# Layer norms of two hybrid layers: GpSimd applies the learned scale and offset for all tiles but the last two of each layer

## The chip, the cores and the metric

One core of a Trainium2 chip. The metric is the device time of one execution in microseconds (us), lower is better. The kernel before takes 3786.14 us, the median of 3 runs.

## The reference, cut to what matters

Four layers run one after the other on 1024 tokens of width 1024: an attention layer, a state-space layer, and two hybrid layers. The change is at the end of each hybrid layer, where the mixed branches `y` are projected and the result is normalised:

```python
def layer_norm(x, g, b):
    xf = x.astype(F32)
    mu = jnp.mean(xf, axis=-1, keepdims=True)
    var = jnp.mean(jnp.square(xf - mu), axis=-1, keepdims=True)
    return ((xf - mu) * lax.rsqrt(var + LN_EPS) * g + b).astype(x.dtype)

def hybrid_layer(...):
    ...
    y = jnp.concatenate([y_conv, y_ret, y_na], axis=-1) @ w_out
    x_new = layer_norm(DEEPNORM_ALPHA * x + gate[:, None] * y, ln_g, ln_b)
    if not need_ctx:
        return x_new, None
    ...
    yc = jnp.concatenate([yc_conv, yc_ret, yc_na], axis=-1) @ w_out
    xc_new = layer_norm(DEEPNORM_ALPHA * xc + mod_c[2] * yc, ln_g, ln_b)
    return x_new, xc_new
```

`ln_g` and `ln_b` have 1024 values each, one per column, the same for every token. Layer 0 normalises 1024 tokens and 256 context tokens, layer 1 the 1024 tokens alone. All data is fp32.

## The kernel before

Rows of tokens lie on the 128 partitions, so a tile is 128 tokens by 1024 columns. Layer 0 (`l == 0`) has 10 tiles (8 of tokens, 2 of context), layer 1 has 8. A projection in fp32 is three matmul passes, over high and low parts of both operands; GpSimd makes the two parts of each slab of weights (`split`, lines 2312 and 2315; `keep`, lines 2425 and 2427, for the six slabs that stay resident), each a 128x1024 instruction.

Each engine runs a program of its own, in the order in which it is written, and waits for semaphores. For the end of a hybrid layer these are `ln_pe`, `ln_act` and `ln_dve`; GpSimd has no part in it. It has finished the slabs of `w_out` by then, and its next work is `split` for the first two slabs of the layer that follows, which waits until the last tile's matmuls have freed their buffers.

**TensorE** (`ln_pe`). `res_first` multiplies tiles 0 to 3 together. Then, in layer 0: tile(4), turn(0), turn(1), tile(5), turn(2), turn(3), tile(6), turn(4), tile(7), turn(5), tile(8), turn(6), tile(9), turn(7), turn(8), turn(9). `tile(t)` is one tile's projection (line 416, 48 matmuls) and from tile 6 on waits for the gating product of tile t-2 (`f_scaled`), which frees its PSUM banks. `turn(t)` is eight transposes of the normalised tile (line 446); it waits for the tile's sum (`f_sum`) and, from tile 2 on, for both takes of tile t-2. In layer 1 there is no turn: tile(4) to tile(7) follow at once.

**VectorE** (`ln_dve`). `gated(t)` is L2083, product of the projection in PSUM and the gate; L2087, plus ALPHA times x with the row sums; L2090, minus the mean. L2087 waits for the rows of x (`f_loaded`). From tile 4 on L2083 waits until the store of tile t-2 has landed. `normed(t)` is L2095, reciprocal of the root; L2097, add and multiply by the two row statistics; L2099, times the learned scale; L2101, plus the learned offset. `take(t)` (L471) and `rest(t)` (L478) write the transposed tile for the next layer.

**ScalarE** (`ln_act`). `square(t)` is L2001, the sum of squares, and L2004, the root. `store(t)` waits for `f_sum`, issues the tile's store (L2009) and, behind it in the same queue, the load of x for tile t+2 (L1996):

```python
def store(t):
    act.wait_ge(f_sum, base + t + 1)
    act.dma_start(orows(t), L_T[:, t % 4]).then_inc(f_stored[t % 2], 16)
    if t + 2 < tiles:
        load_x(t + 2)
```

Its order in both layers starts square(0), square(1), store(0), square(2), store(1), square(3), store(2), store(3). Layer 0 goes on with take(0), take(1), then square(4), take(2), store(4), square(5), take(3), store(5) and so on; a take on ScalarE is L456 and the cast L461. Layer 1 goes on with square(4), store(4), square(5), store(5) and so on.

VectorE's order in both layers starts gated(0), gated(1), normed(0), gated(2), normed(1), gated(3), normed(2), normed(3). Layer 0 goes on with take(0), rest(0), take(1), rest(1), then gated(4), take(2), normed(4), rest(2) and so on. Layer 1 goes on with gated(4), normed(4), gated(5), normed(5) and so on.

Of the kernel before, what the change touches and what calls it, by code (L numbers as in the profile page):

```python
# [16 lines left out]
ALU = mybir.AluOpType  # L17
# [8 lines left out]
NT = S // P  # L26
# [102 lines left out]
T_DONE, F_DONE, Y_DONE = 2 * NT, 2 * NT, KT  # L129
CONST_DONE, FC_DONE = 5, 2  # L130
# [3 lines left out]
def build(nc, io, out):  # L134
    x_in = io["x"].rearrange("b s d -> (b s) d")
    ctx = ExitStack()
    with ctx:
# [3 lines left out]
        def sem(name):  # L141
            return ctx.enter_context(nc.semaphore(name))
# [22 lines left out]
        def region(at, *shape):  # L165
            n = int(np.prod(shape))
            assert at + n <= ARENA, (at, shape)
            v = arena[:, at:at + n]
            if len(shape) == 2:
                v = v.rearrange("p (a b) -> p a b", a=shape[0])  # L170
            if len(shape) == 3:
                v = v.rearrange("p (a b c) -> p a b c", a=shape[0], b=shape[1])
            return v
# [186 lines left out]
        def y_dve(dve, base, src, order8, cols=S):  # L360
# [9 lines left out]
        f_const = sem("f_const")  # L370
        r_mul, f_square, f_root, f_rstd, f_scaled, f_sum = [
            sem(n) for n in ("r_mul", "f_square", "f_root", "f_rstd", "f_scaled", "f_sum")]
# [12 lines left out]
        def ps_tile(j):  # L385
            return psum[:, 2 * j:2 * j + 2, :].rearrange("p a c -> p (a c)")
# [52 lines left out]
        def pair_of(t):  # L439

            return ps_tile(t if t < 4 else t % 2)
# [21 lines left out]
        def take_dve(dve, n, first, gain, full=N_FULL):  # L463

            b = n % 2
            dve.wait_ge(t_turned, n + 1)
            if n >= first + 2:
                dve.wait_ge(t_hi, n - 1)
                dve.wait_ge(t_lo, n - 1)
            for k in range(4, 8):  # L470
                ins = nc.vector.tensor_scalar(full[:, b, k * P:(k + 1) * P], ps_tile(2 + b)[:, k * P:(k + 1) * P],  # L471
                                              gain[:, 0, k:k + 1], gain[:, 1, k:k + 1], ALU.mult, ALU.add)
            ins.then_inc(t_full_dve, 1)

        def rest_dve(dve, n, c0, full=N_FULL):

            dve.wait_ge(t_hi, n + 1)
            nc.vector.tensor_tensor(act_lo[:, :, c0:c0 + P], full[:, n % 2].rearrange("p (k c) -> p k c", k=KT),  # L478
                                    act_hi[:, :, c0:c0 + P].bitcast(F32), ALU.subtract).then_inc(t_lo, 1)
# [1453 lines left out]
        L_T = region(2048, 4, 1024)  # L1933
        RES_L = resident("res_l", *(10240 + 2048 * i for i in range(6)))
        F_GATE = region(22528, 2, 1024)
        F_LN = region(24576, 2, 1024)
# [1 line left out]
        F_SQ = region(28672, 1024)  # L1938
        F_ST2 = region(29696, 4, 8)
        ALPHA = 4.0 ** 0.25  # L1940
        f_chain, f_norm = sem("f_chain"), sem("f_norm")
        def ln_rows(tok, con):
            return lambda t: tok[t * P:(t + 1) * P, :] if t < NT else con[(t - NT) * P:(t - NT + 1) * P, :]

# [46 lines left out]
        def ln_act(act, l, xrows, orows):  # L1991
# [72 lines left out]
            for b in range(2):  # L2064
                act.wait_ge(f_stored[b], 16 * ((base + tiles) // 2))

        def ln_dve(dve, l):

            V = nc.vector
            base, n0 = F_DONE + 10 * l, T_DONE + 10  # L2070
            r0 = 3 * NT + 10 * l

            def half_of(t):
                return pair_of(t) if l == 0 else ps_tile(t % 4)

            def gated(t):
                m, st = base + t, F_ST2[:, t % 4]
                dve.wait_ge(r_mul, r0 + t + 1)
                if t >= 4:
                    dve.wait_ge(f_stored[t % 2], 16 * (m // 2))  # L2080
                    if l == 0:
                        dve.wait_ge(t_turned, n0 + t - 3)
                V.tensor_tensor(L_T[:, t % 4], half_of(t), F_GATE[:, 0 if t < NT else 1], ALU.mult).then_inc(f_scaled, 1)  # L2083
                dve.wait_ge(f_scaled, m + 1)
                dve.wait_ge(f_loaded[t % 2], 16 * (m // 2 + 1))
                k = 2 * (m - F_DONE)
                V.scalar_tensor_tensor(L_T[:, t % 4], L_X[:, t % 2], ALPHA, L_T[:, t % 4], ALU.mult, ALU.add,  # L2087
                                       accum_out=st[:, 0:1]).then_inc(f_chain, 1)
                dve.wait_ge(f_chain, k + 1)
                V.tensor_scalar(st[:, 1:2], st[:, 0:1], -1.0 / D, None, ALU.mult).then_inc(f_chain, 1)  # L2090

            def normed(t):
                m, st = base + t, F_ST2[:, t % 4]
                dve.wait_ge(f_root, m + 1)
                V.reciprocal(st[:, 5:6], st[:, 4:5]).then_inc(f_rstd, 1)  # L2095
                dve.wait_ge(f_rstd, m + 1)
                V.tensor_scalar(L_T[:, t % 4], L_T[:, t % 4], st[:, 1:2], st[:, 5:6], ALU.add, ALU.mult).then_inc(f_norm, 1)  # L2097
                dve.wait_ge(f_norm, 2 * (m - F_DONE) + 1)
                V.tensor_tensor(L_T[:, t % 4], L_T[:, t % 4], F_LN[:, 0], ALU.mult).then_inc(f_norm, 1)  # L2099
                dve.wait_ge(f_norm, 2 * (m - F_DONE) + 2)  # L2100
                V.tensor_tensor(L_T[:, t % 4], L_T[:, t % 4], F_LN[:, 1], ALU.add).then_inc(f_sum, 1)  # L2101

            def take(t):
                take_dve(dve, n0 + t, n0, G_X if t < NT else G_C, L_FULL)

            def rest(t):
                rest_dve(dve, n0 + t, t * P, L_FULL)

            dve.wait_ge(f_const, 16 * (FC_DONE + 4 * (l + 1)))
            gated(0)  # L2110
            gated(1)
            normed(0)
            gated(2)
            normed(1)
            gated(3)
            normed(2)
            normed(3)
            if l == 0:
                take(0)
                rest(0)  # L2120
                take(1)
                rest(1)
                gated(4)
                take(2)
                normed(4)
                rest(2)
                gated(5)
                take(3)
                normed(5)
                rest(3)  # L2130
                gated(6)
                take(4)
                normed(6)
                rest(4)
                gated(7)
                take(5)
                normed(7)
                rest(5)
                gated(8)
                take(6)  # L2140
                normed(8)
                rest(6)
                gated(9)
                take(7)
                normed(9)
                rest(7)
                take(8)
                rest(8)
                take(9)
                rest(9)  # L2150
            else:
                gated(4)
                normed(4)
                gated(5)
                normed(5)
                gated(6)
                normed(6)
                gated(7)
                normed(7)
# [140 lines left out]
        def _(pool):  # L2300
# [8 lines left out]
            def split(m, par):  # L2309
                pool.wait_ge(slot_loaded[par], 16 * m + 16)  # L2310
                pool.wait_ge(slot_used, 2 * m + (par + 1))
                G.tensor_tensor(w_hi[:, par], w_raw[:, par], one[:, 0:1].to_broadcast([P, 1024]),  # L2312
                                ALU.mult).then_inc(slot_hi, 1)
                pool.wait_ge(slot_hi, 2 * m + (par + 1))
                G.tensor_tensor(w_lo[:, par], w_raw[:, par], w_hi[:, par].bitcast(F32),  # L2315
                                ALU.subtract).then_inc(slot_split, 1)
# [93 lines left out]
            def ring(first, last):  # L2410

                with pool.Fori(first // 2, last // 2) as m:
                    for par in range(2):
                        split(m, par)

            def keep(slot0, res, stage):

                for k in range(2):
                    split(slot0 // 2, k)
                pool.wait_ge(stage_done, 3 * stage)  # L2420
                for k in range(2, KT):
                    n = slot0 + k
                    hi, lo = res[k - 2]
                    pool.wait_ge(slot_loaded[k % 2], 16 * (n // 2) + 16)
                    G.tensor_tensor(hi[:, :], w_raw[:, k % 2], one[:, 0:1].to_broadcast([P, 1024]), ALU.mult).then_inc(slot_hi, 1)
                    pool.wait_ge(slot_hi, n + 1)
                    G.tensor_tensor(lo[:, :], w_raw[:, k % 2], hi[:, :].bitcast(F32), ALU.subtract).then_inc(slot_split, 1)
# [7 lines left out]
            for l in range(2):  # L2435
                ring(SLOT_L3[l], SLOT_L3[l] + 32)
                keep(SLOT_L3[l] + 32, RES_L, 8 + 2 * l)


        @block.tensor  # L2440
# [946 lines left out]
```

## Time and profile before

| | |
|---|---|
| median of 3 runs | 3786.14 us |
| lowest, highest | 3785.95, 3790.16 us |
| span of the profiled execution (first to last instruction) | 3789.7 us |
| VectorE busy over the span | 1988.2 us, 52% |
| GpSimd busy over the span | 1228.7 us, 32% |

The profile is of one execution; its span is the only time that is recorded for it, and nothing outside the span is. Times in rows are microseconds from the start of the span. A line such as L2083 is that line of the kernel before. In a chain of waits, each row is what the next one was released by. "idle before" in brackets is how long the engine had stood and what ended it.

### The profile page before, as it was taken

The numbers are of one execution on the slowest core, as the hardware profiler recorded it, in microseconds if no ns is written. First come the engines' busy times: TensorE is split into PE (matmuls) and PEld (weight loads), VectorE is DVE, ScalarE is ACT, GpSimd is POOL, SyncE is SP. The second block draws the span as 40 slices with busy tenths as digits, with TensorE's granted clock in tenths as the row PEclk, the third lists the DMA queues.
The fourth block names the chain that finished last, engine by engine and source line by source line (L and its number), as shares of the span: only waits on it lengthen the run. The fifth ranks groups of instructions, "written<-read, shape, count | busy, mean of one in ns | idle before, by whom it ended". The sixth has DMA issues, their size and how long they took to land.

```text
span 3789.7 us, 50939 instructions
## 1 busy us (share of the span) xinstructions
PE 3478.7 (92%) x19952; PEld 2743.9 (72%) x19952; DVE 1988.2 (52%) x3841; ACT 1252.3 (33%) x2770; POOL 1228.7 (32%) x573
## 2 busy tenths in 40 slices
PE   5989999999999977898389899999998899999998
PEld 4767777777777755666367687788887677788876
DVE  3466557465554657339632524465445734464555
ACT  4434434444443433210031412234332322234331
POOL 1356666333232314448034122211125022211241
PEclk9999999999999978899689999999999999999999
DMA  5212111243322212233243310100002221110113
GB/s 143 49 34 64 57 50 55 72 122 88 98 79 73 68 45 95 80 116 124 71 156 106 110 34 23 29 23 27 19 23 84 100 60 29 28 29 23 28 40 122
DMA packets 312832, 253.37 MB, mean 67 GB/s; under 512 B 64725, under 2 KB 285929, under 8 KB 312602
## 3 DMA queue, kind: packets, MB, share of 16 engines
q1 hardware_dynamic: 202398, 122.48, 11.2%
q10 hardware_dynamic: 110204, 127.70, 10.6%
q8 instruction: 159, 2.61, 0.3%
q14 instruction: 71, 0.58, 0.1%
HBM read 213.75 MB, written 47.99 MB: 69 GB/s over the span
## 4 chain that ended last, share of the span: by engine, by line
PE 76%; DVE 15%; issue 3%; ACT 3%; DMA 2%; SPq 1%; ACTq 0%; POOL 0%; DVEq 0%; POOLq 0%
PE psum L1373 20%; PE psum L2464 19%; PE psum L416 11%; PE psum L1493 3%; PE psum L339 2%; PE psum L2521 2%; PE psum L2476 2%; PE psum L1475 2%; PE psum L2528 2%; PE psum L1485 2%; PE psum L2501 1%; PE psum L1477 1%; DVE arena L3322 1%; DVE arena L3323 1%; PE psum L1404 1%
## 5 line engine op out<-in xcount | busy, mean ns | idle before, releaser
L2312 POOL TENSOR_TENSOR w_hi<-w_raw,one 128x1024 fp32r<-128x1024 f32 x186 | 399.1, 2146 | 2176.8 <-PE psum L1373 1076.6
L1373 PE MATMUL psum<-act_hi,w_hi 128*128 128x512 f32 (+1 forms) x1376 | 517.0, 376 | 11.9 <-DVEq L195 11.9
L2464 PE MATMUL psum<-act_hi,w_hi 128*128 128x512 f32 x1280 | 509.6, 398 | 12.3 <-ACTq L2695 5.8
L2464 PE MATMUL psum<-act_lo,w_hi 128*128 128x512 f32 x1280 | 516.8, 404 | 0.0
L1373 PE MATMUL psum<-act_lo,w_hi 128*128 128x512 f32 (+1 forms) x1376 | 516.5, 375 | 0.0
L1373 PE MATMUL psum<-act_hi,w_lo 128*128 128x512 f32 (+1 forms) x1376 | 514.2, 374 | 0.0
L2464 PE MATMUL psum<-act_hi,w_lo 128*128 128x512 f32 x1280 | 508.5, 397 | 0.0
L2315 POOL TENSOR_TENSOR w_lo<-w_raw,w_hi 128x1024 fp32r<-128x1024 f32 x186 | 478.2, 2571 | 14.6
L1373 PEld LDWEIGHTS psum<-act_hi,w_hi 128*128 128x128 f32 x1376 | 260.8, 190 | 54.5 <-DVEq L195 12.7
L3108 DVE CUSTOM_DVE_ANT_0 arena<-psum,arena 128x128 f32<-128x128 f32 (+1 forms) x384 | 120.2, 353 | 339.6 <-issue 226.8
L1373 PEld LDWEIGHTS psum<-act_lo,w_hi 128*128 128x128 f32 x1376 | 260.7, 189 | 42.9 <-issue 5.0
L1373 PEld LDWEIGHTS psum<-act_hi,w_lo 128*128 128x128 f32 x1376 | 260.5, 189 | 42.5 <-issue 4.0
L2464 PEld LDWEIGHTS psum<-act_hi,w_hi 128*128 128x128 f32 x1280 | 243.2, 190 | 65.3 <-ACTq L195 6.2
L2464 PEld LDWEIGHTS psum<-act_lo,w_hi 128*128 128x128 f32 x1280 | 243.3, 190 | 54.9 <-issue 6.7
L2464 PEld LDWEIGHTS psum<-act_hi,w_lo 128*128 128x128 f32 x1280 | 243.5, 190 | 46.6
L2731 ACT ACTIVATE arena<-arena 128x128 f32<-128x128 f32 (+1 forms) x384 | 170.2, 444 | 299.8 <-DVE arena L3113 299.7
L1124 ACT ACTIVATE arena<-psum 128x512 f32<-128x512 f32 x144 | 135.8, 943 | 127.7 <-PE psum L2464 96.3
L3120 DVE COPY arena<-psum 128x384 f32<-128x384 f32 x192 | 106.1, 553 | 132.5 <-PE psum L2528 132.2
L1493 PEld LDWEIGHTS psum<-arena 128*128 128x128 f32 x1200 | 148.4, 191 | 7.6 <-ACT arena L1680 0.7
L2746 ACT COPY arena<-psum 128x256 f32<-128x256 f32 (+1 forms) x192 | 92.2, 480 | 186.6 <-PE psum L2501 180.4
L1493 PE MATMUL psum<-arena 128*128 128x128 f32 x1200 | 151.5, 275 | 0.0
L1680 ACT COPY arena<-psum 128x768 f32<-128x768 f32 (+1 forms) x108 | 81.2, 752 | 158.5 <-PE psum L1485 157.6
(375 smaller groups left out, 6285.4 us busy)
## 6 DMA issues: line engine op xcount, KB each, us to landing
w_raw<-in_attn_w_in SPq DMA_DIRECT2D x80, 512.0 KB, 3.7
w_raw<-in_w_in SPq DMA_DIRECT2D x64, 512.0 KB, 4.0
spare<-in_w_mod ACTq DMA_DIRECT2D x24, 1024.0 KB, 7.8
w_raw<-in_ssm_w_in SPq DMA_DIRECT2D x32, 512.0 KB, 3.4
x<-arena ACTq DMA_DIRECT2D x24, 512.0 KB, 2.9
arena<-x ACTq DMA_DIRECT2D x24, 512.0 KB, 4.7
arena<-in_x ACTq DMA_DIRECT2D x16, 512.0 KB, 5.3
w_raw<-in_w_out SPq DMA_DIRECT2D x16, 512.0 KB, 3.2
```

The lines of the kernel that those rows point to most:

```text
L416: ins = nc.tensor.matmul(psum[:, bank + c, :], a[:, k, t * P:(t + 1) * P], w[:, c * 512:(c + 1) * 512], start=(k == 0 and w is hi and a is ...
L1124: return nc.scalar.activation(dst, src, ACT.Copy, scale=SCALE if p % 3 == 0 else 1.0)
L1373: ins = nc.tensor.matmul(psum[:, n % 2, 0:c], w[:, slot % 2, k * P:(k + 1) * P], a[:, k, c0:c0 + c], start=(m == 0), stop=(m == 23))
L1493: ins = nc.tensor.matmul(psum[:, 7, 256:384], VR2[:, t], PT2[n % 2][:, i * P:(i + 1) * P], start=(a == 0), stop=(a == len(tiles) - 1))
L1680: C.copy(PT2[n % 2][:, c0:768], flat(6, 2)[:, c0:768]).then_inc(u_pt, 1)
L2312: G.tensor_tensor(w_hi[:, par], w_raw[:, par], one[:, 0:1].to_broadcast([P, 1024]), ALU.mult).then_inc(slot_hi, 1)
L2315: G.tensor_tensor(w_lo[:, par], w_raw[:, par], w_hi[:, par].bitcast(F32), ALU.subtract).then_inc(slot_split, 1)
L2464: ins = nc.tensor.matmul(psum[:, h % 2, :], w[:, (3 + j) % 2, k * P:(k + 1) * P], a[:, k, c:c + 512], start=(m == 0), stop=(m == 23))
L2731: nc.scalar.activation(lg, lg, ACT.Exp, bias=STAT[:, n % 2, 4 + h:5 + h], accum_out=STAT[:, n % 2, h:h + 1]).then_inc(u_probs, 1)
L2746: nc.scalar.copy(PT[:, n % 2, :].rearrange("p (h c) -> p h c", h=2)[:, :, 0:nk * P], psum[:, 4 + n % 2, :].rearrange("p (h c) -> p h c", h ...
L3108: nc.vector.tensor_tensor_reduce(LOG[:, n % 2, h * 256:h * 256 + P * nk], psum[:, 2 + h, 0:P * nk], BIAS[:, h, bias_cols(g, u)], 1.0, -3e3 ...
L3120: nc.vector.tensor_copy(QKV[:, b:b + 3, u * P:(u + 1) * P], psum[:, OB(n), 0:3 * P].rearrange("p (a c) -> p a c", a=3)).then_inc(u_evac, 1)
```

## The change

GpSimd gets a program `ln_pool` for each hybrid layer, which follows the splits of the layer's last weights. For tiles 0 to 7 of layer 0 and 0 to 5 of layer 1 it waits for the normalised tile (`f_norm`), multiplies it by the scale, waits for itself (`f_mul`), adds the offset and raises `f_sum`. VectorE's `normed` returns after L2097 for these tiles. For the last two tiles of a layer VectorE does both steps as before, with one more wait, that the sum of the tile before is there. The tiles are updated in place, as before. The splits for the layer that follows come after `ln_pool` in GpSimd's program.

```diff
--- before.py
+++ after.py
@@ -1938,7 +1938,7 @@
         F_SQ = region(28672, 1024)
         F_ST2 = region(29696, 4, 8)
         ALPHA = 4.0 ** 0.25
-        f_chain, f_norm = sem("f_chain"), sem("f_norm")
+        f_chain, f_norm, f_mul = sem("f_chain"), sem("f_norm"), sem("f_mul")
         def ln_rows(tok, con):
             return lambda t: tok[t * P:(t + 1) * P, :] if t < NT else con[(t - NT) * P:(t - NT + 1) * P, :]
 
@@ -2064,11 +2064,22 @@
             for b in range(2):
                 act.wait_ge(f_stored[b], 16 * ((base + tiles) // 2))
 
+        def ln_pool(pool, l):
+
+            base = F_DONE + 10 * l
+            pool.wait_ge(f_const, 16 * (FC_DONE + 4 * (l + 1)))
+            for t in range(NT - 2 * l):
+                pool.wait_ge(f_norm, (NT + 4) * l + t + 1)
+                nc.gpsimd.tensor_tensor(L_T[:, t % 4], L_T[:, t % 4], F_LN[:, 0], ALU.mult).then_inc(f_mul, 1)
+                pool.wait_ge(f_mul, NT * l + t + 1)
+                nc.gpsimd.tensor_tensor(L_T[:, t % 4], L_T[:, t % 4], F_LN[:, 1], ALU.add).then_inc(f_sum, 1)
+
         def ln_dve(dve, l):
 
             V = nc.vector
             base, n0 = F_DONE + 10 * l, T_DONE + 10
             r0 = 3 * NT + 10 * l
+            shared = NT - 2 * l
 
             def half_of(t):
                 return pair_of(t) if l == 0 else ps_tile(t % 4)
@@ -2095,9 +2106,13 @@
                 V.reciprocal(st[:, 5:6], st[:, 4:5]).then_inc(f_rstd, 1)
                 dve.wait_ge(f_rstd, m + 1)
                 V.tensor_scalar(L_T[:, t % 4], L_T[:, t % 4], st[:, 1:2], st[:, 5:6], ALU.add, ALU.mult).then_inc(f_norm, 1)
-                dve.wait_ge(f_norm, 2 * (m - F_DONE) + 1)
+                if t < shared:
+                    return
+                n = (NT + 4) * l + shared + 2 * (t - shared)
+                dve.wait_ge(f_norm, n + 1)
                 V.tensor_tensor(L_T[:, t % 4], L_T[:, t % 4], F_LN[:, 0], ALU.mult).then_inc(f_norm, 1)
-                dve.wait_ge(f_norm, 2 * (m - F_DONE) + 2)
+                dve.wait_ge(f_norm, n + 2)
+                dve.wait_ge(f_sum, m)
                 V.tensor_tensor(L_T[:, t % 4], L_T[:, t % 4], F_LN[:, 1], ALU.add).then_inc(f_sum, 1)
 
             def take(t):
@@ -2435,6 +2450,7 @@
             for l in range(2):
                 ring(SLOT_L3[l], SLOT_L3[l] + 32)
                 keep(SLOT_L3[l] + 32, RES_L, 8 + 2 * l)
+                ln_pool(pool, l)
 
 
         @block.tensor
```

## Rows read from the trace of the kernel before

**Rows 1.** The page of the profiled execution: its span, and the first of its busy times.

```profile
span 3789.7 us, 50939 instructions
...
PE 3478.7 (92%) x19952; PEld 2743.9 (72%) x19952; DVE 1988.2 (52%) x3841; ACT 1252.3 (33%) x2770; POOL 1228.7 (32%) x573
```

**Rows 2.** The chain of waits, layer 0: start us, length us, what held it.

```profile
2936.83 0.82 DVE arena L2097
...
2937.68 1.24 DVE arena L2099
...
2940.19 0.33 ACTq L2009
...
2945.71 1.25 DVE arena L2087 x2
...
2956.86 0.83 DVE arena L2097
...
2963.67 0.33 ACTq L2009
...
2971.95 1.23 DVE arena L2083
...
2973.23 13.93 PE psum L416 x48
...
2988.03 11.18 PE psum L416 x48
...
3023.32 1.23 DVE arena L2083
```

**Rows 3.** The chain of waits, layer 1, same columns.

```profile
3748.20 0.83 DVE arena L2097
...
3751.56 0.34 ACTq L2009
...
3756.53 1.25 DVE arena L2087 x2
...
3759.79 0.82 DVE arena L2097
...
3765.75 1.25 ACT arena L2001 x2
...
3773.51 1.25 ACT arena L2001 x2
```

**Rows 4.** GpSimd's instruction groups by form, 1960 to 2030: busy us, mean ns.

```profile
L927 POOL TENSOR_TENSOR arena<-arena 128x1024 f32<-128x1024 f32 x8 | 19.1, 2398 | 45.1 <-DMA arena<-z_rows 45.1
```

**Rows 5.** GpSimd's timeline, layer 0: start us, length us, line, operation.

```profile
3021.73 1.89 POOL L2312 TENSOR_TENSOR w_hi<-w_raw,one 128x1024 fp32r<-128x1024 f32 x1 [106.34 <-PE psum L416]
3023.70 2.36 POOL L2315 TENSOR_TENSOR w_lo<-w_raw,w_hi 128x1024 fp32r<-128x1024 f32 x1
3026.02 2.88 POOL L2312 TENSOR_TENSOR w_hi<-w_raw,one 128x1024 fp32r<-128x1024 f32 x1
3028.98 2.34 POOL L2315 TENSOR_TENSOR w_lo<-w_raw,w_hi 128x1024 fp32r<-128x1024 f32 x1
```

**Rows 6.** VectorE's timeline, the same stretch.

```profile
3024.58 2.57 DVE L2087 SCALAR_TENSOR_TENSOR arena<-arena 128x1024 f32<-128x1024 f32 x1
...
3029.18 2.69 DVE L2097 TENSOR_SCALAR arena<-arena 128x1024 f32<-128x1024 f32 x1
```

**Rows 7.** TensorE's timeline, layer 0.

```profile
2986.99 1.04 PE L446 MATMUL psum<-ident,arena 128*128 128x128 f32 x8
```

**Rows 8.** ScalarE's timeline, one row of each layer.

```profile
2979.82 0.33 ACTq L2009 DMA_DIRECT2D x<-arena  x1
...
3763.53 0.45 ACTq L1996 DMA_DIRECT2D arena<-x  x1
```

**Rows 9.** DMA issues, 3720 to 3790: count, size, median us to landing.

```profile
out_dram<-arena ACTq DMA_DIRECT2D x8, 512.0 KB, 2.9
```

**Rows 10.** Windows: length, PE, PEld, DVE, ACT, POOL busy, granted clock, DMA share, GB/s.

```profile
2966.00:2979.00 13.00, 8.81 (x30) 7.01 (x31) 10.21 (x18) 7.50 (x15) 0.00 (x0) 0.61 0.12 40
```

## The prediction

> **What bounds the kernel now.** The busy shares [rows 1] come first: TensorE is busy for 92% of the span. That says little here, because the edit touches two stretches of about 110 and 64 us, and each has its own limit. So the second view is the chain of waits in each.
>
> Layer 0 [rows 2]. Up to 2971.95 the chain alternates between VectorE and transfers: the multiply and add of tile 0 (from 2937.68) end, ScalarE's queue issues store(0) at 2940.19 and right behind it load_x(2), and VectorE's L2087 for tile 2 starts when those rows of x land, at 2945.71. The same happens for tile 3. The reader should see that the sum of a tile (f_sum) gates not just its store but, through the order of ScalarE's queue, the load of x two tiles on. Store(3) at 2963.67 also stands ahead of take(0) on ScalarE, and take(0), take(1) stand ahead of gated(4) on VectorE, for which TensorE's tile(6) waits until 2973.23. From there TensorE sets the end (tiles 6 to 9) until 3023.32; then comes a VectorE and ScalarE tail.
>
> Layer 1 [rows 3]. The same load waits, the last one before L2087 of tile 4 at 3756.53, then a serial round per tile, L2083, L2087, square, root, L2097, L2099, L2101: the squares of tiles 5 and 6 start at 3765.75 and 3773.51, a period of 7.76 us. It ends the kernel.
>
> **Time base.** The span of the profiled execution is 3789.7 us, 3.6 over the median of the runs (3786.14) and 0.5 below the highest (3790.16). I work out a difference in the trace and add it to the median.
>
> **The change, priced.** It removes L2099 and L2101 from VectorE for 8 + 6 tiles and gives GpSimd two instructions per tile. On VectorE the pair and the hand-on to store(0) take 2.51 us, from 2937.68 to 2940.19 [rows 2]. GpSimd has the same form (128x1024, two full fp32 inputs from SBUF) at L927: 8 of 2.398 us [rows 4]. The split at L2312 is cheaper, 1.89 us, but its second input is one broadcast column; L2315 with two full inputs takes 2.34 to 2.36 [rows 5]. I take 2.40. With 0.08 us from one GpSimd instruction to the next [rows 5] and some 0.06 to start and hand on, norm to store takes 0.06 + 2.40 + 0.08 + 2.40 + 0.05 = 4.99 us, where VectorE's way takes 2.55 (L2097 ends by 2937.65, store 2940.19 [rows 2]). So a sum is 2.44 us later.
>
> Sharing. In the tail of layer 0 GpSimd's splits of the next layer meet VectorE [rows 5, 6]. L2087 (two SBUF inputs) at 3024.58 takes 2.57 instead of about 1.2 us: L2315 had started first, and L2087 ends 1.09 us after it. The L2312 behind it then takes 2.88 instead of 1.89. L2097, whose only full input is in SBUF, takes 2.69 instead of 0.82 and ends 0.55 us after L2315. L2083, which reads PSUM, keeps its 1.23 beside L2312 [rows 2]. So the two engines take turns, an instruction at a time, and a waiting VectorE instruction gets in between two of GpSimd. The Trainium skill (SBUF — State Buffer, "Who interferes with whom") says so too: whoever issues first holds the shared ports and the other fully blocks. Its trace analysis page (Perfetto Trace Analysis, "Optimizing Scalar/DVE Operations") draws the conclusion against this change, that moving work between these two engines might not help. The rows above agree and my sum contains this; the rival without it is below.
>
> Layer 0, step by step:
> (a) store(0), so load_x(2), so L2087 of tile 2: +2.44. VectorE's freed time buys nothing, since it waits there for the load [rows 2].
> (b) normed(1) is behind gated(2) on VectorE, so sum 1, store(1), load_x(3): another +2.44, now +4.88.
> (c) L2097 of tile 2 starts at 2956.86 + 4.88 = 2961.74 and ends at 2962.56. GpSimd multiplies to 2965.0; L2097 of tile 3 is held meanwhile and ends 0.55 later, at 2965.55; then add 2 to 2967.95, multiply 3 to 2970.45, add 3 to 2972.9. Store(3) goes at 2972.95 instead of 2963.67: +9.3.
> (d) take(0) on ScalarE, take and rest 0 and 1, gated(4), tile(6) follow store(3) as before: +9.3.
> (e) From tile(6) on, TensorE has no slack to give back. Does GpSimd add more? turn(4) needs sum 4. Before, gated(4)'s L2083 at 2971.95 led to store(4) at 2979.82, 7.9 us; with 2.44 more and an L478 that gets between (1.2) it is 11.5, at 2992.8, and turn(4) would start at 2986.99 + 9.3 = 2996.3 [rows 2, 7, 8]. Cover 3.5 us; without it each us would be on the path. Later sums have a whole further TensorE tile ahead of their turn. So zero.
> (f) The tail is tiles 8 and 9, still on VectorE. GpSimd's splits come behind ln_pool in its program; they start when tile(9) frees their buffers, and sum 7 can start two tiles of TensorE before that. Zero; if it were late, a split pair of 4.3 us [rows 5] would slide into the next layer.
> Layer 0: **+9.3**.
>
> Layer 1:
> (g) The two load waits again: +4.88.
> (h) L2097 of tile 2 ends at 3749.0 + 4.88 = 3753.9 [rows 3]; multiply to 3756.35, L2097 of tile 3 ends 3756.9, add to 3759.3, store(2) at 3759.35 instead of 3751.56, +7.8. Load_x(4) is issued behind it, so L2087 of tile 4 starts at 3764.3 (before 3756.53): +7.8. The store's landing (2.9 us [rows 9]), for which gated(4) waits, falls before that.
> (i) ScalarE's order is square(4), store(4), square(5). L2097 of tile 4 ends at 3760.6 + 7.8 = 3768.4; multiply to 3770.85; L2087 of tile 5 gets in to 3771.9; add to 3774.3; store and load issue take 0.85 (0.34 and 0.45 and the gaps [rows 3, 8]); square(5) starts at 3775.2 instead of 3765.75: +9.45.
> (j) Once more for tile 5: L2097 ends 3777.8, multiply 3780.25, L2087 of tile 6 to 3781.3, add 3783.7, square(6) at 3784.6 instead of 3773.51: +11.1. Tiles 6 and 7 run as before.
> Layer 1: **+11.1**.
>
> Sum 9.3 + 11.1 = **+20.4 us**, so 3786.1 + 20.4 = 3806.5.
>
> TensorE's clock: around the stop before tile(6) it is granted 0.61 on average (full being 2.4 GHz, the lower level 1.2) [rows 10]. The first 48 matmuls then hold the chain for 13.93 us, where the later sets of 48 in it take about 11.2 (2973.23 and 2988.03 [rows 2]): 2.7 us, which are in the base. The stop gets longer by up to 9 us; if that cost a second such set, it is 0 to +2.7. I take 0, since the engine is already at its low level there.
>
> **Rivals.**
> R1, the other side: the wait on GpSimd is short enough that VectorE's freed 2.5 us per tile decide. If GpSimd's pair took VectorE's 2.5 us and nobody were held, (a), (b) are zero, L2097 of tile 3 (0.85) is hidden in layer 0, and in layer 1 square(t+1) would start 0.05 + 2.5 + 0.85 = 3.4 us after norm(t) instead of 5.15, gaining 1.75 twice: 0.9 + 3.5 = 4.4 us, 3781.7. It decides from about 1.3 us per GpSimd instruction. No row of this size is below 1.89. Chance 0.03.
> R2, no blocking between the two engines: (c) loses 0.55, (i), (j) and (h) lose about 2.4: +17.5, 3803.6. Against it stands the turn-taking [rows 5, 6]. Chance 0.12.
> R3, more blocking: VectorE gets in front of nearly each GpSimd instruction, which then takes 3.0 rather than 2.4. Each of the roughly 15 GpSimd instructions on the path (2 + 2 + 4 in layer 0, 2 + 2 + 1 + 2 + 2 in layer 1, some overlapping) gets 0.6 longer, and VectorE's next ones wait on it: +9 to +14, so about 3818. For it: L2312 at 2.88. Against: in (a), (b) VectorE stands idle for its load. Chance 0.12.
> R4, layer 0's delay is hidden: TensorE would do tile(6) in time after all. Then +11.1 alone, 3797.2. Against: it already waits there for gated(4) [rows 2]. Chance 0.07.
> R5, none of it on the path, within 0.2%: the store-to-load order would have to have slack in both layers, which the load waits contradict. Chance 0.03.
> The forecast (3802 to 3812, its own clock term included): 0.63.
>
> **How the numbers follow.** The time is the forecast's, 3806.5. The range takes in R2 and most of R3 and reaches toward R4: 3798 to 3819. 0.2% is 7.6 us, about what a measurement of this kernel can tell from no change. Slower holds the forecast, R2, R3 and R4, 0.94; same is R5, 0.03; faster is R1, 0.03.
>
> **What the profile after would show.** L2099 and L2101 on VectorE 4 times each; 28 new GpSimd instructions of 2.4 us (some 3.4 where held); store(0) 2.4 us and store(3) some 9.3 us later after the stretch opens; tile(6) 9 us later, then the same TensorE rhythm; L2097 of tile 3 about 2 us long; in layer 1 a period near 9.4 us for tiles 4 and 5 and 7.76 afterwards. The prediction is wrong if GpSimd's instructions differ much from 2.4 us, if x loads land at another delay when issued at other moments, or if TensorE's start after the longer stop costs more.

## The result and the profile after

The changed kernel takes 3806.44 us (median of 4 runs, 3805.02 to 3807.68), the kernel before in the same comparison 3788.15 us (4 runs, 3785.95 to 3790.16). The ratio is 1.0050, 95% interval 1.0037 to 1.0063: 14 to 24 us slower. The medians differ by 18.3 us. Forecast were +20.4 us and 3806.5.

The profiled execution of the changed kernel has a span of 3805.3 us and a time of 3807.14. The line numbers move: L2094 is the gating product (L2083 before), L2098 adds ALPHA times x (L2087), L2106 and L2108 are reciprocal and normalisation (L2095, L2097), L2113 and L2116 are VectorE's scale and offset (L2099, L2101). L2073 and L2075 are GpSimd's.

The chain of waits of the changed kernel in layer 0, start us, length us, what held it; it answers to [rows 2]:

```profile
2933.44 0.82 DVE arena L2108
...
2934.39 2.43 POOL arena L2073
...
2936.89 2.41 POOL arena L2075
...
2939.32 0.33 ACTq L2009
...
2943.59 1.25 DVE arena L2098 x2
...
2956.94 0.82 DVE arena L2108
...
2960.31 2.72 POOL arena L2075
2963.03 2.36 POOL arena L2073
...
2965.46 2.35 POOL arena L2075
...
2967.83 0.33 ACTq L2009
...
2976.11 1.23 DVE arena L2094
...
2977.38 13.57 PE psum L416 x48
...
3027.11 1.24 DVE arena L2094
```

GpSimd's two instructions (2934.39, 2936.89) now stand between VectorE's L2108 and store(0) at 2939.32. Measured from the first gating product of the stretch (2930.97 before, 2927.58 here), store(0) goes at 11.74 us instead of 9.22. For tiles 2 and 3 four GpSimd instructions lie end to end up to store(3) at 2967.83, 40.25 us into the stretch instead of 32.70. From tile(6) on (2977.38) the chain is TensorE's again, with the same 48-matmul pieces, and the gating product of tile 9 at 3027.11 is no further away than before.

VectorE's timeline in the same stretch:

```profile
2943.59 1.23 DVE L2098 SCALAR_TENSOR_TENSOR arena<-arena 128x1024 f32<-128x1024 f32 x1 [8.21 <-DMA arena<-x]
...
2958.67 2.11 DVE L2108 TENSOR_SCALAR arena<-arena 128x1024 f32<-128x1024 f32 x1
...
2980.62 0.81 DVE L2108 TENSOR_SCALAR arena<-arena 128x1024 f32<-128x1024 f32 x1
2982.90 2.10 DVE L478 TENSOR_TENSOR act_lo<-arena,act_hi 128x1024 fp32r<-128x1024 f32 x1 [1.46 <-ACT act_hi L461]
...
2986.16 2.17 DVE L2098 SCALAR_TENSOR_TENSOR arena<-arena 128x1024 f32<-128x1024 f32 x1
```

L2098 of tile 2 waits 8.21 us for the load of x; all that VectorE no longer does is in that wait. L2108 of tile 3 takes 2.11 us instead of 0.81: GpSimd's multiply of tile 2 (2957.83 to 2960.23) had started first, and L2108 ends 0.55 us behind it. In the part that TensorE sets, VectorE's L478 (both inputs in SBUF) takes 2.10 us and ends at 2985.00, GpSimd's add of tile 4 runs behind it until 2987.25, and L2098 of tile 5 behind that takes 2.17 us. GpSimd's timeline:

```profile
2983.99 3.26 POOL L2075 TENSOR_TENSOR arena<-arena 128x1024 f32<-128x1024 f32 x1
2991.27 2.40 POOL L2073 TENSOR_TENSOR arena<-arena 128x1024 f32<-128x1024 f32 x1 [4.02 <-DVE arena L2108]
```

An add that VectorE gets in front of takes 3.26 us, a multiply that nobody disturbs 2.40. Of the 28 new GpSimd instructions none is under 2.34.

The chain of layer 1; it answers to [rows 3]:

```profile
3733.15 2.41 POOL arena L2073
...
3738.43 4.36 DMA arena<-x
...
3750.60 5.76 DMA arena<-x
...
3764.11 0.34 ACTq L2009
...
3769.20 1.25 DVE arena L2098 x2
...
3775.81 3.21 POOL arena L2075
...
3779.91 1.25 ACT arena L2001 x2
...
3789.14 1.25 ACT arena L2001 x2
```

Squares of tiles 5 and 6 start at 3779.91 and 3789.14, 9.23 us apart where it was 7.76, each behind a GpSimd add (3775.81, 3.21 us long) and the store and load issue.

Both traces cut at the same events, in us:

| stretch | before | after | difference | forecast |
|---|---|---|---|---|
| layer 0: first gating product to store(0) | 9.22 | 11.74 | +2.52 | +2.44 |
| to VectorE's add of x, tile 2 | 5.52 | 4.27 | -1.25 | 0 |
| to store(1) | 4.89 | 7.22 | +2.33 | +2.44 |
| to add of x, tile 3 | 4.73 | 4.60 | -0.13 | 0 |
| to store(3) | 8.34 | 12.42 | +4.08 | +4.42 |
| to gating product of tile 4 | 8.28 | 8.28 | 0 | 0 |
| to gating product of tile 9 | 51.37 | 51.00 | -0.37 | 0 |
| to the next layer's first matmul | 19.64 | 19.65 | +0.01 | 0 |
| **layer 0** | 111.99 | 119.18 | **+7.2** | +9.3 |
| layer 1: first gating product to store(0) | 9.16 | 11.96 | +2.80 | +2.44 |
| to add of x, tile 2 | 5.16 | 4.83 | -0.33 | 0 |
| to store(1) | 4.89 | 7.33 | +2.44 | +2.44 |
| to add of x, tile 3 | 4.83 | 6.23 | +1.40 | 0 |
| to store(2) | 4.89 | 7.66 | +2.77 | +2.92 |
| to add of x, tile 4 | 4.97 | 5.09 | +0.12 | 0 |
| to square(5) | 9.22 | 10.71 | +1.49 | +1.65 |
| to square(6) | 7.76 | 9.23 | +1.47 | +1.65 |
| to the last sum | 12.88 | 12.88 | 0 | 0 |
| **layer 1** | 63.76 | 75.92 | **+12.2** | +11.1 |

Together +19.4 us. The spans differ by 15.6 only: the rest of the program, the same code in both, is 3613.9 us before and 3610.2 after. Nearly all of that difference lies ahead of the first changed instruction: layer 0's first gating product starts at 2930.97 before and at 2927.58 after. Over the nine profiles of this study that rest lies between 3608.0 and 3615.4, while the two stretches repeat to 0.8 us where the code is the same. So small effects are read below from the stretches, with the timed ratio beside them.

### The profile page after: what moved, and what is told of

It is laid out like the page before. It is cut to its first block, busy times and chain, and to the rows that moved or that the text cites. A ratio compares the mean times of both kernels' runs of the same rounds, so it can differ in the third digit from the quotient of the medians.

```text
span 3805.3 us, 50945 instructions
## 1 busy us (share of the span) xinstructions
PE 3474.5 (91%) x19952; PEld 2741.3 (72%) x19952; DVE 1964.6 (52%) x3813; ACT 1252.6 (33%) x2770; POOL 1300.8 (34%) x601
## 3 DMA queue, kind: packets, MB, share of 16 engines
q1 hardware_dynamic: 202398, 122.48, 11.1%
## 4 chain that ended last, share of the span: by engine, by line
PE 75%; DVE 14%; issue 4%; ACT 3%; DMA 1%; POOL 1%; ACTq 0%; DVEq 0%; POOLq 0%
PE psum L1373 20%; PE psum L2480 19%; PE psum L416 11%; PE psum L1493 3%; PE psum L339 2%; PE psum L2537 2%; PE psum L2492 2%; PE psum L1475 2%; PE psum L2544 2%; PE psum L1485 2%; PE psum L2517 1%; PE psum L1477 1%; DVE arena L3338 1%; DVE arena L3339 1%; PE psum L1404 1%
```

## The experiments

All are compared with the kernel before. Stretch times are those of the table's bold rows, from one trace of each kernel.

**1. Layer 0 alone.** On the changed kernel, in `ln_pool` and `normed`, with the semaphore counts to match:

```diff
+        GP_TILES = ([0, 1, 2, 3, 4, 5, 6, 7], [])
...
-            for t in range(NT - 2 * l):
+            for i, t in enumerate(GP_TILES[l]):
...
-                if t < shared:
+                if t in GP_TILES[l]:
                     return
```

> GpSimd takes tiles 0 to 7 of layer 0 only; layer 1 is as in the kernel before. Theory (late sums delay the x loads of tiles 2 and 3 and then take(0), by 2.44 + 2.44 + 4.43 us; TensorE hides the rest): +7 to +9.5 us over before. Rival A (the loss is the two engines blocking each other, so it goes with the number of tiles moved, 8 of 14): +10 to +11.5.

Measured: 3797.27 against 3788.95 us, ratio 1.0022 (1.0013 to 1.0031), +8.3 us. Stretches: layer 0 119.28 (+7.3), layer 1 63.65 (-0.1). The timed interval, +5 to +12 us, holds both the theory and rival A; the stretch speaks for the theory.

**2. Layer 1 alone.** The same edit with `GP_TILES = ([], [0, ..., 5])`.

> GpSimd takes tiles 0 to 5 of layer 1 only. Theory: +11 to +12.5 us over before, more than layer 0 although two tiles fewer are moved. Rival A (by the number of tiles, 6 of 14): +8 to +9.

Measured: 3801.12 against 3788.95 us, ratio 1.0033 (1.0021 to 1.0045), +12.2 us. Stretches: layer 0 112.09 (+0.1), layer 1 75.17 (+11.4). By the stretches six tiles cost more than eight, and the two parts add up to the whole. That is against a loss by the number of tiles. The times alone (+8 to +17 us here) would not settle it.

**3. Layer 0, tiles 4 to 7 alone.** `GP_TILES = ([4, 5, 6, 7], [])`.

> GpSimd takes only tiles 4 to 7 of layer 0, where TensorE holds the chain. Theory: the sums are later by 3 to 5 us each but have 3.5 us or more of cover, so 0 (within 1.5 us of before). Rival A (by the number of tiles, 4 of 14): +5 to +6. The profile should show VectorE's L2087 and the rest near 2.1 us in these tiles all the same, and no change of TensorE's rhythm.

Measured: 3788.87 against 3788.95 us, ratio 1.0002 (0.9993 to 1.0011), which leaves no room for rival A. Layer 0 takes 111.65 us (-0.3). The chain of waits of this kernel has TensorE's pieces as before:

```profile
2968.68 14.16 PE psum L416 x48
...
2983.71 11.16 PE psum L416 x48
```

and VectorE's timeline shows the add of x (L2102 here) of tile 4 undisturbed and that of tile 5 held by GpSimd:

```profile
2968.66 1.22 DVE L2102 SCALAR_TENSOR_TENSOR arena<-arena 128x1024 f32<-128x1024 f32 x1
...
2977.50 2.18 DVE L2102 SCALAR_TENSOR_TENSOR arena<-arena 128x1024 f32<-128x1024 f32 x1
```

It is nearly a microsecond longer, and nothing on the chain waits for it: here, where TensorE sets the pace, late sums and blocked instructions cost nothing. Half of layer 0's moved tiles are free, so its whole loss is in tiles 0 to 3.

**4. The changed kernel with early loads.** In `ln_act` of the changed kernel:

```diff
             def square(t):
...
                                      bias=ln_eps[:, 0:1]).then_inc(f_root, 1)
+                if t + 2 < tiles:
+                    load_x(t + 2)
...
             def store(t):
                 act.wait_ge(f_sum, base + t + 1)
                 act.dma_start(orows(t), L_T[:, t % 4]).then_inc(f_stored[t % 2], 16)
-                if t + 2 < tiles:
-                    load_x(t + 2)
```

square(t) has already waited for VectorE's use of x of tile t, so the buffer is free there.

> The changed kernel, with x of tile t+2 loaded right behind square(t) on ScalarE's queue, not behind store(t). Theory: takes the load waits and their +4.9 us per layer away; GpSimd itself then limits tiles 0 to 3 (8 instructions of 2.4 us and some five turns of about 1 us for VectorE), so 3784 to 3789, some 20 us under the changed kernel. Rival A (blocking is the loss): still 12 us or more over before, 3798 or more. Rival B (the loads are late for another reason, bandwidth): no change, 3806.

Measured: 3782.04 against 3788.95 us, ratio 0.9985 (0.9976 to 0.9994), 6.9 us under before and 24 under the changed kernel; somewhat below the range that was expected, and far from both rivals. Stretches: layer 0 108.44, layer 1 62.30, against 119.18 and 75.92 with late loads. VectorE's timeline in layer 1 shows what is left:

```profile
3722.45 2.75 DVE L2098 SCALAR_TENSOR_TENSOR arena<-arena 128x1024 f32<-128x1024 f32 x1
...
3743.70 1.23 DVE L2094 TENSOR_TENSOR arena<-psum,arena 128x1024 f32<-128x1024 f32 x1 [6.26 <-DMA out_dram<-arena]
...
3756.86 0.16 DVE L2106 RECIPROCAL arena<-arena 128x1 f32<-128x1 f32 x1 [4.08 <-ACT arena L2004]
```

The add of x of tile 2 has its rows, but is held 1.5 us by GpSimd; the gating product of tile 4 waits 6.26 us for the landing of store(2), which is late because the sum is; and the reciprocal waits 4.08 us for a root whose square stood behind store(4).

**5. The kernel before with early loads.** The same edit on the kernel before.

> The kernel before (VectorE does all of it) with x of tile t+2 loaded right behind square(t). Theory: the five load waits (4.4 and 3.6 us in layer 0; 4.1, 3.7 and 0.4 us in layer 1) go, 13 to 16 us under before, so 3773 to 3776, and below the changed kernel with the same loads (3782): GpSimd's slower sums cost 6 to 9 us even then. Rival (with the loads early, moving work off VectorE is a gain): this kernel is no faster than 3782.

Measured: 3772.85 against 3788.62 us, ratio 0.9958 (0.9945 to 0.9972), 15.8 us faster, the fastest kernel here. Stretches: layer 0 102.63 (-9.4), layer 1 56.67 (-7.1). VectorE's timeline, layer 1, the add of x of tile 2 (L2087) and the gating product of tile 7 (L2083):

```profile
3725.09 1.23 DVE L2087 SCALAR_TENSOR_TENSOR arena<-arena 128x1024 f32<-128x1024 f32 x1
...
3763.62 1.23 DVE L2083 TENSOR_TENSOR arena<-psum,arena 128x1024 f32<-128x1024 f32 x1 [0.90 <-PE psum L416]
```

No VectorE instruction waits for x any more, L2087 keeps its 1.23 us, and a limit shows that did not before: TensorE has only just finished tile 7 (0.90 us). Against experiment 4, GpSimd's part costs 5.8 us in layer 0 and 5.6 in layer 1 also when the loads are early.

**6. GpSimd adds, VectorE multiplies.** On the changed kernel. VectorE keeps the scale; GpSimd waits for that and adds the offset.

```diff
                 V.tensor_tensor(L_T[:, t % 4], L_T[:, t % 4], F_LN[:, 0], ALU.mult).then_inc(f_norm, 1)
+                if t < shared:
+                    return
                 dve.wait_ge(f_norm, n + 2)
```

> As the changed kernel, but VectorE multiplies by the scale and GpSimd only adds the offset, for the same 14 tiles. Theory (the loss is the lateness of the sum): a sum is 1.2 us later, not 2.44; by the same steps +4.5 us in layer 0 and +3.6 in layer 1, so +8 over before (range +6 to +10), well under half of the changed kernel's 20. Rival A (the loss is per handing over or per blocking, not per us of lateness): +12 to +20.

Measured: 3799.08 against 3788.62 us, ratio 1.0027 (1.0016 to 1.0038), +10.5 us, just above the expected range by the medians; the stretches give +3.5 (115.44) and +3.6 (67.32), +7.0 together. The timed interval (+6 to +14 us) leaves room for the low end of the rival; the stretches leave none. By them the loss is a little over a third of the full change's 19.4 us, where the sum is late by about half as much. In layer 0 part of the smallness is fortune with the loads: the two took 3.95 and 4.41 us from issue to landing, against 5.07 and 4.27 in the trace of before, and with those times the loss would be about +4.4, close to the expected +4.5. So the loss goes with the lateness of the sum, but holding has a part: on the chain VectorE's normalisation of tile 3 (L2106 here) is held by GpSimd's add of tile 2 and takes 2.92 us instead of 0.82.

```profile
2959.74 2.92 DVE arena L2106
```

**7. Early loads, and the square first.** On the kernel of experiment 4, in layer 1 of `ln_act`:

```diff
                 square(4)
-                store(4)
                 square(5)
-                store(5)
+                store(4)
                 square(6)
-                store(6)
+                store(5)
                 square(7)
+                store(6)
                 store(7)
```

> The changed kernel with early loads, and in layer 1 square(t+1) stands ahead of store(t) on ScalarE's queue for tiles 4 to 6. Theory (steps i and j: square behind the store waits on GpSimd's sum): 2 to 4 us under the changed kernel with early loads alone (3782), the waits of VectorE for the root in tiles 5 and 6 fall from 4.1 to under 2.5 us, and the landing of the store becomes the next wait. Rival (the order doesn't matter, VectorE or GpSimd is the bound): 3782, within 1 us.

Measured: 3781.12 against 3788.62 us, ratio 0.9981 (0.9972 to 0.9990). The median is 0.9 us under that of experiment 4, less than the 2 to 4 us that were expected and within the rival's 1 us. The timed ratios of experiments 4 and 7 overlap and don't separate them, so what follows rests on one trace of each. The stretch of layer 1 is 60.32 against 62.30, 2.0 us less, with layer 0 the same (108.46 and 108.44). VectorE's timeline, the reciprocal of tile 5 and the gating product of tile 6:

```profile
3752.80 0.16 DVE L2106 RECIPROCAL arena<-arena 128x1 f32<-128x1 f32 x1 [1.64 <-ACT arena L2004]
...
3757.97 1.23 DVE L2094 TENSOR_TENSOR arena<-psum,arena 128x1024 f32<-128x1024 f32 x1 [4.16 <-DMA out_dram<-arena]
```

The wait for the root is 1.64 us instead of 4.08, as it was with VectorE alone; the same reciprocal in the kernel before:

```profile
3767.35 0.16 DVE L2095 RECIPROCAL arena<-arena 128x1 f32<-128x1 f32 x1 [1.64 <-ACT arena L2004]
```

The landing of store(4) is the next wait, 4.16 us. So the wait that (i) and (j) describe comes from the order of the queue, and with the order changed most of what is saved is spent on the next wait.

## Why the prediction was right, step by step

**The price.** 2.40 us per GpSimd instruction was read from a multiply of the same form [rows 4], and the new instructions take 2.34 to 2.42 where undisturbed. Each of the first tiles' sums comes 2.33 to 2.80 us later, forecast 2.44. One row was misread on the way: L2083 at 3023.32 runs mostly beside L2315, which starts at 3023.70, and not beside L2312; it keeps its 1.23 us all the same.

**(a), (b), (g), the load waits.** The mechanism holds: VectorE idles for the load whatever it is freed from, shown by experiments 4 and 5, in which the load waits go and both kernels gain. Its size was mis-set by what the forecast held constant, the time from the issue of a load to its landing. The prediction had named another landing time as a sign of being wrong, and it occurred. The loads on the chain before, two of each layer:

```profile
2940.55 5.07 DMA arena<-x
...
2950.96 4.27 DMA arena<-x
...
3732.17 4.69 DMA arena<-x
...
3742.22 4.35 DMA arena<-x
```

and after:

```profile
2939.68 3.82 DMA arena<-x
...
2951.17 4.15 DMA arena<-x
...
3738.43 4.36 DMA arena<-x
...
3750.60 5.76 DMA arena<-x
```

So these steps measured +3.5 in layer 0 and +6.3 in layer 1 instead of +4.9 twice. With the differences in the rows "to add of x" taken out, layer 0 would be +8.6 and layer 1 +11.0, near the forecast's +9.3 and +11.1. The opposite signs of these two errors are luck, and so is much of the fit of 3806.5 to 3806.44: the forecast started from a median of 3786.14 us, 2.0 below the 3788.15 of the comparison, and its +20.4 is 2.1 above the 18.3 by which the medians differ. What made single loads faster or slower was not tried; a trace of it is under the last heading.

**(c), (h), the turns.** +4.08 for +4.42 and +2.77 for +2.92. The sum charged a held VectorE instruction its full 0.55 us on top of the add; the add, having started to wait, ended 0.32 us late (2.72 against 2.40).

**(d).** Exactly as forecast: 8.28 us from store(3) to gated(4) in both.

**(e), cover.** Right, and tested alone by experiment 3. In the changed kernel sum 4 is ready 11.2 us after the gating product of tile 4 starts (2976.11 to store(4) at 2987.28), forecast 11.5; turn(4) starts behind tile(6) at 2990.95.

**(f), the tail.** 19.64 and 19.65 us.

**(i), (j), ScalarE's order.** +1.49 and +1.47 for +1.65 each. Experiment 7 shows the mechanism in its trace; its time doesn't show it.

**TensorE's clock.** No second set of slow matmuls: the first piece of 48 takes 13.57 us in the changed kernel, after the longer stop, and 13.93 in the kernel before. The granted clock is at its lower level, 0.50, when tile(6) starts in both kernels (2970 to 2976 before, 2970 to 2980 after) and full, 1.00, from 2979 and from 2983. So the 0 that the forecast took for the clock is right.

**The rivals.** R1 (VectorE's freed time decides) is refuted by the result, and with early loads too VectorE alone is faster (experiments 5 and 4). R2 (no blocking) is refuted by the 2.11 and 2.17 us rows; its +17.5 us lies inside the timed interval, so the time alone would not have told it from the forecast. R4 (layer 0 hidden) falls by experiment 1, R5 (none of it on the path) by the interval of the result. R3 (more blocking) is half seen: adds do take 3.2 us once VectorE has its loads, but in layer 0 from tile 4 that costs nothing, and in layer 1 it is what (i) and (j) had charged.

## What to carry to other kernels

Before work is moved off an engine, look at what that engine does with the time: here VectorE waited for loads of x, and the moved steps were the ones that released those loads. When a load is issued behind a store in one queue, every delay of the result delays the load too, and a later tile pays for it; so issue the load where its buffer comes free. That alone gave 15.8 us on the kernel before, nearly as much as the change lost. The slower engine took its work for nothing here only where a third engine set the pace and the result had slack, in tiles 4 to 7 of layer 0.

## What was not expected of the hardware

The landing time of equal 512 KB loads varied from 3.8 to 5.8 us between and within executions, which is as large as the effect per tile that was being forecast. The traces show two things that go with it. The load of 5.07 us (2940.55, before) has a long issue on ScalarE's queue, 1.26 us where the next one has 0.45:

```profile
2940.55 1.26 ACTq L1996 DMA_DIRECT2D arena<-x  x1
...
2950.96 0.45 ACTq L1996 DMA_DIRECT2D arena<-x  x1
```

The load of 5.40 us in experiment 2 has one of 1.22 us too; in experiment 3 the issue takes 0.99 us and the landing still 4.33.

And the three landings on the chains above 5.1 us (5.76 in the changed kernel, 5.40 and 5.52 in experiment 2) have a packet of the kind "instruction" moving while they are under way. For the changed kernel, 3750.20 to 3756.36 (packets, MB, share):

```profile
q8 instruction: 1, 0.02, 0.9%
```

Of the other loads on the chains of the kernels with late loads only one, of 4.35 us in experiment 6, has such a packet beside it. So the loading of the program may be what slows single loads; no run tries it.

The first GpSimd instruction of layer 1 in the changed kernel started 0.4 us after VectorE's L2108 ended (3732.72 to 3733.15), where the others of the first tiles took 0.07 to 0.14. It is 0.4 us in experiments 4 and 7 too, and 0.14 in experiments 2 and 6; the cause is open.
